# The two rate products of the next pair go directly behind the recurrence's own products, the bonus product between the transposes

## What is computed

```python
r, k, v, xw, xa, xg = jnp.split(Pm, ...)
w_log = -jax.nn.softplus(-(w0 + jnp.tanh(xw) @ w2)) - 0.5
decay = jnp.exp(-jnp.exp(w_log))
a = jax.nn.sigmoid(a0 + xa @ a2)
k = k * (1.0 + (a - 1.0) * k_a)
# scan over time, per head: S = S*w + (S a) b + v k ;  y = S r
y, S = _wkv_scan(rh, decay, kh, vh, -kk, kk * ah, S0)
bonus = jnp.sum(rh * kh * r_k, axis=-1, keepdims=True) * vh
out = (yn + bonus) * g
```

## Time and profile before

| | us |
|---|---|
| median of three runs | 797.09 |
| the three runs | 793.96, 797.09, 797.59 |
| the profiled execution, whole | 792.39 |
| its span, first to last instruction | 790.5 |
| TensorE busy in it | 744.4 (94%) |
| VectorE busy | 444.3 (56%) |
| ScalarE busy | 239.2 (30%) |

### The profile page before, as it was taken

How to read it: one execution, slowest core, us unless ns; L and a number is a source line. 1 busy time by engine, 2 the same in 40 slices (tenths; PEclk the granted TensorE clock), 3 DMA queues, 4 the chain that set the end, 5 groups by cost and what they waited for, 6 DMA issues and landing times.

```text
span 790.5 us, 18161 instructions
## 1 busy us (share of the span) xinstructions
PE 744.4 (94%) x7060; PEld 462.2 (58%) x7060; DVE 444.3 (56%) x1172; ACT 239.2 (30%) x591; POOL 61.2 (8%) x71
## 2 busy tenths in 40 slices
PE   4999999999999999999999999999899999998874
PEld 4666666666666666666666666454555555554431
DVE  3364677777777767767867865516423432232226
ACT  4234343353452552453444443221000001000012
POOL 3000000400000000000000000000131312222100
PEclk9999999999999999999999999999999999999997
DMA  9343142771160160251151551897999999999975
GB/s 243 106 114 110 28 125 80 136 196 32 27 188 13 45 180 11 60 161 27 46 156 27 198 189 45 305 393 284 369 412 409 420 418 419 421 408 420 404 284 192
DMA packets 116838, 160.06 MB, mean 202 GB/s; under 512 B 27858, under 2 KB 92172, under 8 KB 110120
## 3 DMA queue, kind: packets, MB, share of 16 engines
q1 hardware_dynamic: 100244, 147.57, 52.2%
q0 software_dynamic: 5760, 7.80, 3.8%
q10 hardware_dynamic: 10789, 4.06, 2.0%
HBM read 154.43 MB, written 15.73 MB: 215 GB/s over the span
## 4 chain that ended last, share of the span: by engine, by line
PE 79%; DMA 9%; SPq 3%; DVE 3%; ACT 2%; issue 2%; POOL 0%; ACTq 0%; POOLq 0%; DVEq 0%
PE bank L790 24%; PE bank L1200 9%; PE bank L961 5%; PE bank L1095 4%; PE bank L796 4%; PE bank L1039 4%; PE bank L1207 4%; DMA vecs<-in_exp_up 2%; DMA shared<-in_exp_up 2%; DMA ybuf<-vecs,sidx 2%; PE bank L894 2%; PE bank L762 2%; PE bank L903 2%; PE bank L824 1%; PE bank L1229 1%
## 5 line engine op out<-in xcount | busy, mean ns | idle before, releaser
L790 PE MATMUL bank<-xnT,wall 128*128 128x320 f32 x656 | 195.4, 442 | 2.4 <-ACT vecs L1391 2.4
L790 PEld LDWEIGHTS bank<-xnT,wall 128*128 128x128 f32 x656 | 118.5, 189 | 49.1 <-issue 4.9
L681 POOL DMA_INDIRECT merged<-xn2d,gidx x15 | 15.5, 1035 | 520.2 <-DVE gidx L2102 411.8
L2146 DVE COPY vecs<-bank 128x512 f32<-128x512 f32 x32 | 22.1, 690 | 59.4 <-DMA ybuf<-vecs,sidx 32.3
L961 PE MATMUL bank<-xnT,wall 128*128 128x320 f32 x128 | 47.9, 456 | 0.3
L2151 DVE TENSOR_TENSOR scratch<-bank,n 128x512 f32<-128x512 f32 x30 | 20.5, 686 | 49.0 <-PE bank L1200 45.4
L1200 PE MATMUL bank<-vecs,scratch 128*64 128x256 f32 x352 | 41.8, 391 | 5.6 <-DMA vecs<-in_exp_up 5.1
L1602 ACT ACTIVATE vecs<-bank 128x128 f32<-128x128 f32 x32 | 8.9, 277 | 119.4 <-PE bank L1200 119.4
L1200 PE MATMUL bank<-scratch 128*64 128x256 f32 x320 | 36.7, 382 | 2.2 <-DMA scratch<-in_exp_up 1.8
L1200 PEld LDWEIGHTS bank<-vecs,scratch 128*64 128x64 f32 x352 | 25.4, 141 | 18.5 <-DMA vecs<-in_exp_up 5.7
L1370 ACT ACTIVATE shared<-bank 128x256 f32<-128x256 f32 x32 | 12.3, 385 | 73.5 <-PE bank L790 66.8
(11 more groups left out here) (426 smaller groups left out, 1352.0 us busy)
## 6 DMA issues: line engine op xcount, KB each, us to landing
wall<-in_w_in SPq DMA_DIRECT2D x58, 512.0 KB, 5.3
vecs<-in_exp_gate SPq DMA_DIRECT2D x11, 1024.0 KB
vecs<-in_exp_up SPq DMA_DIRECT2D x11, 1024.0 KB
scratch<-in_exp_gate SPq DMA_DIRECT2D x10, 1024.0 KB
scratch<-in_exp_up SPq DMA_DIRECT2D x10, 1024.0 KB
scratch<-in_exp_down SPq DMA_DIRECT2D x6, 1024.0 KB
shared<-in_exp_gate SPq DMA_DIRECT2D x10, 512.0 KB
shared<-in_exp_up SPq DMA_DIRECT2D x10, 512.0 KB
```

The source lines that it names most:

```text
L790: q = mm(tpbank(L, name), wbuf[name][:, k, :], xnT[:, k, :], start=(k == 0), stop=(k == KC - 1))
L2146: CP(ye[:, e % 2, :], bank[6 + e % 2][:]).then_inc(S("ye"), 1)
```

## The change

`zw` and `za` of the next pair move directly behind the own products, and `bon` moves from there to their old place between the two fours of transposes. ScalarE reads them in the new order, and `TURN` lists them so. In the last turn, where there are no rate products, `bon` moves behind the first four transposes too.

```diff
--- before.py
+++ after.py
@@ -41,7 +41,7 @@
 
 
 NEXT = ("zw", "r", "za", "k", "v", "ss", "lx")
-TURN = [("ly", "a"), ("bon", "a"), ("zw", "a"), ("za", "a"), ("r", "a"), ("k", "a"), ("v", "a"), ("gl", "a"),
+TURN = [("ly", "a"), ("zw", "a"), ("za", "a"), ("bon", "a"), ("r", "a"), ("k", "a"), ("v", "a"), ("gl", "a"),
         ("gx", "a"), ("ga", "a"), ("ss", "d"), ("g", "d"), ("gr", "a"), ("mean", "d"), ("lx", "a"), ("var", "a")]
 
 
@@ -829,14 +829,15 @@
                 own(3, 1).then_inc(S("big"), 1)
                 own(4, 0)
                 own(4, 1).then_inc(S("big"), 1)
-                pe.wait_ge(S("rkk"), i + 1)
-                single(L, i, "bon", blk, rkk[:])
+                if not last:
+                    zw(L, i, i + 1)
+                    za(L, i)
 
                 for j in range(2):
                     b, c0 = bank[5 + j], 128 * j
-                    if j and not last:
-                        zw(L, i, i + 1)
-                        za(L, i)
+                    if j:
+                        pe.wait_ge(S("rkk"), i + 1)
+                        single(L, i, "bon", blk, rkk[:])
                     for e in range(2):
                         tr(b[:, 128 * e:128 * e + 128], stacked(2 * j + e), ident)
                     tr(b[:, 384:512], vm[:, 128 - c0:256 - c0], ident)
@@ -1418,12 +1419,13 @@
                 A(ysq[:], tpbank(L, "ly"), ACT.Square)
                 A(ysb[:], tpbank(L, "ly"), ACT.Copy).then_inc(S("taken_a"), 1)
 
-                tp_ready(act, L, i, "bon")
-                A(bsum, tpbank(L, "bon"), ACT.Copy).then_inc(S("taken_a"), 1)
+                if not last:
+                    rate_in(L, i, i + 1)
+                    rate(L, i, i + 1)
                 for j in range(2):
-                    if j and not last:
-                        rate_in(L, i, i + 1)
-                        rate(L, i, i + 1)
+                    if j:
+                        tp_ready(act, L, i, "bon")
+                        A(bsum, tpbank(L, "bon"), ACT.Copy).then_inc(S("taken_a"), 1)
                     b = bank[5 + j]
                     act.wait_ge(S("tm_ps"), i * 3 + (j + 1))
                     A(TM[:, 384 * j:384 * j + 384], b[:, 0:384], ACT.Copy)
```

## The result

The changed kernel takes 788.88 us (median of six runs, 787.48 to 790.25) against 795.53 us of the kernel before (six runs beside them, 793.11 to 797.89). The profiled execution has a span of 788.0 us.

| us | before | changed |
|---|---|---|
| preparation | 59.49 | 60.17 |
| turn 0 | 57.51 | 55.77 |
| turns 1 to 6 | 337.86 (56.31 each) | 334.48 (55.74 to 55.77 each) |
| last turn | 41.71 | 43.36 |
| rest | 293.93 | 294.22 |

A forecast was written before the change was run, and what follows sets the result against it. TensorE was taken as the bound (79% of the chain), stalled 2.4 us before r by ScalarE's late tanh of zw. Gains of 1.6 + 0.66 + 0.2 = 2.5 us off 797.09 gave 794.6 us, range 790.8 to 797.8.

The forecast's parts named there:

- the rival in which it does not arrive: End of kernel: a later wait that does not move with TensorE eats the gain, 797.1 us; chance 10%.
- Turn 0: First turn: table load hidden beside TensorE's own products, r at 63.40 instead of 65.03, gain 1.6 us, lower bound 0.35.
- The Trainium skill's drain behind a table load: Turn 0: a page's claim of about 1.38 us drain after the load, 2.66 in all, leaving a gain of 0.3.
- The steady turn: Turns 1 to 6: bon waits 0.17 for zw's tanh, r comes 0.11 us earlier per turn, 0.66 in six.
- its worst bound: Steady turn: late tanh of zw, za's wait for ly adding at most 0.05; loss 0.06 per turn, 0.4 in six.
- "best" bound: Steady turn: no stall at bon, r at 289.84, gain 0.28 us per turn, 1.7 in six.
- The 75% for no change that can be told: Whole kernel: chance that the measured change stays within half a percent, 4.0 us; 20% was given to faster, 5% to slower.
- The first rival: Steady turns: zw is seen earlier than gx was, no wait at bon; 3.6 us gained, 793.5 us; chance 14%.
- The last turn: Last turn: ScalarE's row of copies starts earlier, behind the first four transposes; gain 0.2 us, bounds 0 and 0.25.
- The slower rival: Wait at bon for zw's tanh takes more than the old one; 1.2 us lost, 798.3 us; chance 6%.
- The unhidden load: Turn 0: table load starts only with its product and is not hidden; gain only 1.2 us, 795.9 us; chance 8%.

The follow-up runs named there:

- act_only: Kernel before, ScalarE alone changed to read zw and za directly behind the copy of bon, ahead of both fours; 793.76 against 793.75 us, ratio 1.0002.
- experiment 2: One-column dummy tanh ahead of turn 0, in the kernel before (turn 0 from 57.51 to 56.08 us) and in the changed kernel (55.77 to 55.54).
- four_first: Changed kernel with the first four transposes ahead of zw and za on TensorE, ScalarE reading the pair first; one run, 791.06 us, steady turn 56.11.
- bon_last: Changed kernel with bon behind the second four transposes, so nothing on TensorE waits in time for ScalarE's tanh; ratio 0.9917 to the kernel before.
- pe_only: Changed kernel with ScalarE reading the first four transposes ahead of the tanh of zw and za, TensorE's order kept; 806.29 us, ratio 1.0154.
- after_again: The changed kernel itself run once more, nothing altered; ratio 0.9919 to the kernel before.
- zw_late: Changed kernel with a small one-column tanh on ScalarE between zw and its tanh; one run, 788.34 us, steady turn still 55.75.
- after_early_table: Changed kernel plus a one-column dummy tanh on ScalarE ahead of turn 0; ratio 0.9951 to the kernel before, turn 0 55.54 us.

## Why the prediction was wrong

**What bounds the kernel: the place right, the cause only in turn 0.** The stall is where it was read, and what was taken from TensorE's path arrived at the end, so the rival in which it does not arrive failed. But in a steady turn the tanh was not late by the copies of `bon` and of the first four, as the prediction has it: without the copies of the four ahead of it (`act_only`) it starts only 0.11 earlier. The wait was the round trip itself: 1.70 from `zw` to `r` before, 1.43 from `zw` to `bon` now.

**Turn 0: right, the exact number by luck.** Forecast 1.6, measured 1.63 from the own products to `r` (5.54 to 3.91) and 1.74 in the stage. The load ran where it was put: it began at 61.06, at the end of L1420. But `bon` came 2.85 after the own products instead of 2.74, with a wait of 0.34 where none was expected, and from `bon` to `r` it took 1.06 instead of 1.17; the two cancel. The Trainium skill's drain behind a table load (ScalarE: Activation LUTs, What ACT_TABLE_LOAD costs) is contradicted by both traces: the activation follows the load by 0.01 us, and experiment 2 recovered 1.43 us, not 2.66.

**The steady turn: the term that failed, 0.11 forecast and 0.56 measured.** The mechanism named, a shorter wait at `bon` for the tanh of `zw` in the place of the wait at `r`, is seen in turn 1 and in part in turn 5. In the others the wait is at `za`, for the read of `ly`, to which the prediction gave at most 0.05 in its worst bound; `r` comes at the same time there to within 0.04, so the sum can be compared. Four sizes in it were wrong, all to one side:

- `zw` was set at the place of `bon`, 1.32 after the own products. It begins after 1.22: 0.10.
- The round trip from `zw` to `bon` was put at 0.95 + 0.51 + 0.13 = 1.59, from `gx` and from `r`. It is 0.84 + 0.53 + 0.06 = 1.43: 0.16. `act_only` and `four_first` show that the 0.95 is right behind transposes.
- The second four was given the 0.53 that the first four took ahead of the pair. Behind `bon` and with nothing to wait for, `r` comes after 0.43: 0.10. (In the kernel before the second four stood behind the pair, where a four takes 0.49; the old wait at `r` was so 0.32 and not 0.28.)
- `r`'s own restart out of a wait, 1.34 against 1.24 for its first products, was not in the sum: 0.09.

Together 0.45, which with 0.11 gives 0.56. The common fault: lengths of TensorE's steps were carried from their old neighbours to new ones. The "best" bound of 0.28 per turn had the same fault, so the range was too narrow as well: with no wait at all, turn 1 of `bon_last` takes 0.97 less than before. The 75% for no change that can be told stood on the same sum. The first rival, that the wait is gone for good, fits the page, and its 793.5 was nearer than the forecast; but `bon_last` shows that a wait of 0.40 with what it costs behind it is left in turn 1.

**The last turn: 0.2 forecast, 0.09 at L921, nothing in the stage.** What stood next behind ScalarE was not asked.

**The slower rival: did not happen.** `pe_only` shows that a longer round trip does cost time, 1.5% there, falls of the clock included. **The unhidden load** did not happen either: it stands beside the own products.

**The sums.** The trace gives 5.1 us for the turns, the timing 6.65 with an interval of about 4.7 to 8.4. The control (`after_again`) has medians of 788.60 and 794.33 us, 5.7 apart. What remains is inside the interval and is not settled. Of the 5.7 us between forecast and result, 2.7 are the six steady turns (6 times 0.45), and 1.6 come from the start: the three runs had a median of 797.09, the six beside the result 795.53. The last 1.4 are what the timing shows beyond the trace, less 0.1 by which turn 0 and the last turn together came out below their terms.

## What to carry to other kernels

A step on the path has no length of its own: read it from a place with the same neighbours in front and behind, and where a stall goes, count the restart behind it too. A wait that stands behind short matmuls can vanish from the idle column; compare the distance of two starts with the same distance where nothing waits, or take the wait away and see what the turn becomes. Where a product hangs on another engine's read, move the order on both engines together: here one half alone left the time as it was, and the other lost.

## What was not expected of the hardware

The way from a matmul's start to the activation that reads it was 0.84 to 0.86 us behind the own products and 0.95 behind transposes, for the same product and the same tanh. Two steps of 0.1 would account for all the ways measured here, though neither was tested by itself. One is the pair's bias column in the loop: the tanh without one came 0.74 after `zw` behind the own products (`zw_late`), as did the tanh of `zw` in turn 0 of `after_early_table`, where the column's address is fixed. The other is a product with another number of rows than the one ahead of it: `zw` (64 rows) behind transposes (128), `bon` (128, its copy 0.84 without a bias column) behind the own products (64).

The starts show a step of the same size. Behind the own products `zw` begins after 1.22 and `bon` after 1.32; behind the last transpose `bon` begins after 0.11 and `zw` after 0.20 (`bon_last`, `four_first`). Since either half of the rows does it, what lies behind it stays open.

And a wait of 1.56 us on TensorE was followed, in two of the six steady turns of `pe_only`, by 4 us at a granted clock between 0.54 and 0.61, while the other four, with waits of the same length, kept theirs.
